# The up projection of a feed-forward layer in seven half products in place of eight, with its activations passed through memory

## What is computed

```python
def conv_ffn(xn, ffn_up, ffn_conv_w, ffn_conv_b, ffn_down):
    u = causal_depthwise_conv(xn @ ffn_up, ffn_conv_w, ffn_conv_b)
    gate, up = jnp.split(u, 2, axis=-1)
    return (jax.nn.gelu(gate, approximate=True) * up) @ ffn_down
```

## Time and profile before

| | |
|---|---|
| median of 3 runs | 3038.76 us (3037.23 to 3042.54) |
| profiled execution, its span | 3034.1 us |
| TensorE busy | 2887.8 us, 95% |
| VectorE, ScalarE, GpSimd busy | 53%, 38%, 37% |
| granted TensorE clock, mean | 0.981 |

### The profile page before, as it was taken

The page is one execution under the profiler, slowest core; times in us unless marked ns, Lnnn a source line. Parts: engine busy times, 40 slices in busy tenths (PEclk is TensorE's granted clock), DMA queues, the critical chain, the costliest instruction groups (busy, mean ns, idle before and its releaser), DMA issues.

```text
span 3034.1 us, 43412 instructions
## 1 busy us (share of the span) xinstructions
PE 2887.8 (95%) x15476; PEld 2429.7 (80%) x15476; DVE 1616.0 (53%) x2999; ACT 1160.1 (38%) x2100; POOL 1114.8 (37%) x760
## 2 busy tenths in 40 slices
PE   7999998999999999999999999999999978889999
PEld 6689867777888888887888788997878776778877
DVE  3899938343222222223039378981223849978861
ACT  3311166252222211223123356772312536767740
POOL 2223033532222225663236334335332534333234
PEclk9999997899999999999999999999999999999999
DMA  4123323431111113353856444314436763131223
GB/s 140 64 97 132 97 76 74 132 125 42 48 48 48 48 48 97 119 180 99 160 187 196 108 117 95 105 38 135 145 120 215 206 159 81 49 77 35 83 84 125
DMA packets 219008, 321.37 MB, mean 106 GB/s; under 512 B 81942, under 2 KB 152470, under 8 KB 218342
## 3 DMA queue, kind: packets, MB, share of 16 engines
q1 hardware_dynamic: 195446, 275.20, 31.5%
q10 hardware_dynamic: 22192, 39.98, 3.6%
q0 software_dynamic: 1216, 4.20, 0.5%
HBM read 227.86 MB, written 91.47 MB: 105 GB/s over the span
## 4 chain that ended last, share of the span: by engine, by line
PE 83%; DVE 6%; issue 3%; DMA 2%; ACT 2%; POOL 2%; SPq 1%; POOLq 0%; DVEq 0%; ACTq 0%
PE psum L2783 16%; PE psum L737 13%; PE psum L2568 8%; PE psum L2986 8%; PE psum L444 6%; PE psum L1275 4%; PE psum L1306 4%; PE psum L1286 3%; PE psum L530 3%; PE psum L1573 2%; PE psum L984 2%; PE psum L962 1%; DVE arena L3574 1%; PE psum L973 1%; PE psum L2033 1%
## 5 line engine op out<-in xcount | busy, mean ns | idle before, releaser
L2783 PE MATMUL psum<-parts_ffn 128*128 128x512 f32 x2112 | 482.2, 391 | 3.6 <-DVE parts_ffn L2740 3.6
L2783 PEld LDWEIGHTS psum<-parts_ffn 128*128 128x128 f32 x2112 | 398.5, 189 | 87.1 <-issue 2.2
L2853 DVE SCALAR_TENSOR_TENSOR arena<-psum,arena 128x1023 f32<-128x1023 f32 x88 | 112.9, 1282 | 329.9 <-ACT arena L2837 323.6
L737 PE MATMUL psum<-parts_even,parts_ffn 128*128 128x512 f32 (+1 forms) x1344 | 287.4, 375 | 0.0
L737 PE MATMUL psum<-parts_odd 128*128 128x496 f32 (+1 forms) x1344 | 269.2, 360 | 6.3 <-POOL parts_odd L652 5.4
L737 PEld LDWEIGHTS psum<-parts_even,parts_ffn 128*128 128x128 f32 x1344 | 238.5, 188 | 44.5
L737 PEld LDWEIGHTS psum<-parts_odd 128*128 128x128 f32 x1344 | 226.8, 191 | 41.7 <-POOL parts_odd L652 5.6
L444 PE MATMUL psum<-parts_mixer 128*128 128x512 f32 x912 | 210.4, 391 | 0.3 <-DVE parts_mixer L287 0.3
L444 PEld LDWEIGHTS psum<-parts_mixer 128*128 128x128 f32 x912 | 170.8, 188 | 35.9 <-DVE parts_mixer L287 0.5
L402 POOL CAST parts_ffn<-arena 128x1024 fp32r<-128x1024 f32 x44 | 45.8, 1042 | 355.7 <-PE psum L2783 194.6
L2311 DVE TENSOR_SCALAR_CACHE_REDUCE choose_flags<-arena,choose_bits 128x384 uint8<-128x384 f32 (+2 forms) x198 | 174.3, 942 | 1.2
(11 more groups left out here) (396 smaller groups left out, 5977.9 us busy)
## 6 DMA issues: line engine op xcount, KB each, us to landing
arena<-ffn_up_b SPq DMA_DIRECT2D x44, 512.0 KB, 3.5
arena<-ffn_down_k SPq DMA_DIRECT2D x44, 512.0 KB, 3.7
arena<-x SPq DMA_DIRECT2D x8, 2048.0 KB, 10.1
x<-arena SPq DMA_DIRECT2D x24, 512.0 KB, 4.0
arena<-w_in_e SPq DMA_DIRECT2D x24, 512.0 KB, 5.5
e_tokens<-arena ACTq DMA_DIRECT2D x24, 512.0 KB, 3.7
arena<-w_in_o SPq DMA_DIRECT2D x24, 496.0 KB, 5.9
o_tokens<-arena ACTq DMA_DIRECT2D x20, 496.0 KB, 3.5
```

Of the source, the lines that this page charges most:

```text
L737: last = pe.matmul(self.bank(t, n), self.hT[:, a, k, t * P:(t + 1) * P], w, start=(k, a, b) == (0, 0, 0), stop=(k, a) == (KT - 1, 1))
L2783: last = pe.matmul(self.core.psum[:, 4 * u + 2 * s + h, :], parts[:, s, a, k, :], self.hT[:, b, k, h * HALF:(h + 1) * HALF], start=(k, a, ...
L2853: dve.scalar_tensor_tensor(out=self.cs[:, s, lag:S], in0=src[:, 0:S - lag], scalar=self.conv_w[:, bass.ds(at * 3 + 2 - lag, 1)], in1=self. ...
```

## The change

`FfnUp` is written anew. The weights of a gate and an up tile are cut in two along k: A11 and A12 (gate), A21 and A22 (up); `hT` is cut along k and along the tokens: B11, B21 (first 512 tokens), B12, B22. The four half results C11, C12 (gate), C21, C22 (up) come from seven products of half the k length, in Winograd's form of Strassen's method: sums s1 to s4 of the weights and t1 to t4 of the activations, P1 = A11 B11, P2 = A12 B21, P3 = s4 B22, P4 = A22 t4, P5 = s1 t1, P6 = s2 t2, P7 = s3 t3. Each is 4 k tiles by three matmuls, 12 matmuls of 128x512; a pair has 84. Some are added up in PSUM (P2 on P1; P7 and P4 on P6; P3 on P5), the rest by ScalarE and VectorE into a new SBUF buffer `gu`.

The t blocks are made once, at the opening of the stage (`HalfBlocks`), in place of the plain taking out of the second half of the tokens. The sums of the weights are made for each pair: on GpSimd for the first, on VectorE for the others (`next_sums`, four additions of 128x512), and GpSimd splits seven parts of 128x512 in place of two of 128x1024. The taps read `gu` in SBUF in place of PSUM. A pair's weights (1024 KB) come in one load, and VectorE's result of 128x1024 is stored to memory (`store`, 512 KB) and read back by `FfnDown` in steps of 256 KB (`load_act`). In the loop, body r multiplies pair r (P1, P6, P5, P2, P7, P3) and P4 of pair r-1; VectorE finishes pair r-1 there and makes the sums of pair r+1. On SP, iteration r waits for the split of A22 of pair r-1, loads the weights of pair r+1, waits for the result of pair r-1 and stores it. Buffers have new places, and there are 20 more semaphores.

```diff
...
+        finish(engine, 5)
+        if ahead is not None:
+            ahead(engine)
+        for t in range(6, TT):
             finish(engine, t)
...
+class HalfBlocks:
...
+    def wait_bank(self, pe, k):
+        if k < self.Q:
+            pe.wait_ge(self.rows.low_out, 5 + k)
+        else:
+            self.wait(pe, "t1_raw", k - 4)
+    def keep_first(self, pool):
+        for k in range(KT):
+            high, low = self.first(k)
+            pool.wait_ge(self.rows.low_out, k + 1)
+            if k == self.Q:
+                pool.wait_ge(self.rows.stored[0], 16 * (TT // 2))
+            pool.tensor_tensor(self.plain("t1" if k < self.Q else "t4", k % self.Q), high.bitcast(F32), low.bitcast(F32), ALU.add).then_inc(self.by_gpsimd, 1)
...
+    def vector_second(self, dve):
+        Q = self.Q
+        for k in range(Q):
+            self.wait(dve, "held", k)
+            self.wait(dve, "raw_first", k)
+            dve.scalar_tensor_tensor(out=self.plain("t1", k), in0=self.bank(k), scalar=self.column(k), in1=self.plain("t1", k),
+                                     op0=ALU.mult, op1=ALU.subtract).then_inc(self.by_vector, 1)
+        for k in range(Q):
+            dve.wait_ge(self.rows.turned, KT + Q + k + 1)
+            self.wait(dve, "t1_raw", k)
+            dve.scalar_tensor_tensor(out=self.plain("t2", k), in0=self.bank(k), scalar=self.column(Q + k), in1=self.plain("t1", k),
+                                     op0=ALU.mult, op1=ALU.subtract).then_inc(self.by_vector, 1)
+            self.wait(dve, "t2_raw", k)
+            self.wait(dve, "raw_first", Q + k)
+            dve.tensor_tensor(self.plain("t4", k), self.plain("t4", k), self.plain("t2", k), ALU.subtract).then_inc(self.by_vector, 1)
+        for k in range(Q):
+            self.wait(dve, "t2_high", k)
+            self.wait(dve, "t4_raw", k)
+            dve.tensor_tensor(self.low("t2", k), self.plain("t2", k), self.high("t2", k).bitcast(F32), ALU.subtract).then_inc(self.by_vector, 1)
+        for k in range(Q):
+            self.wait(dve, "b22_high", k)
+            dve.scalar_tensor_tensor(out=self.plain("t3", k), in0=self.bank(k), scalar=self.column(Q + k), in1=self.plain("t3", k),
+                                     op0=ALU.mult, op1=ALU.subtract).then_inc(self.by_vector, 1)
+        for k in range(Q):
+            dve.scalar_tensor_tensor(out=self.low("b22", k), in0=self.bank(k), scalar=self.column(Q + k), in1=self.high("b22", k).bitcast(F32),
+                                     op0=ALU.mult, op1=ALU.subtract).then_inc(self.by_vector, 1)
...
 class FfnUp(Stage):
...
+    TERMS = {"p1": ("a11", "b11", 0), "p2": ("a12", "b21", 0), "p6": ("s2", "t2", 1), "p7": ("s3", "t3", 1),
+             "p4": ("a22", "t4", 1), "p5": ("s1", "t1", 2), "p3": ("s4", "b22", 2)}
+    STARTS = ("p1", "p6", "p5")
+    USER = {weight: product for product, (weight, *_) in TERMS.items()}
...
+    def bodies(self, engine, first=0):
+        for n in range(first, 2):
+            yield n, n - 1, n + 1, 0, (n + 1) // 2, n % 2, n
+        with engine.Fori(0, self.tiles // 2 - 2) as i:
+            for e in range(2):
+                yield 2 * i + (2 + e), 2 * i + (1 + e), 2 * i + (3 + e), i + 1, i + (1 + e), e, None
+        for n in range(self.tiles - 2, self.tiles):
+            yield n, n - 1, n + 1, n // 2, (n + 1) // 2, n % 2, n
+    def bank(self, n, side):
+        return self.core.psum[:, 3 * side + n, :]
...
+    def load(self, sp, r, e):
+        sp.dma_start(self.raw[e].rearrange("p (s a) f -> p s (a f)", s=2), self.w[bass.ds(2 * r, 2)].rearrange("s p f -> p s f")).then_inc(self.loaded[e], 16)
+    def load_first(self, sp):
+        hold(sp, self.retired + self.after["raw0"])
+        self.load(sp, 0, 0)
+    def store(self, sp, q, e):
+        sp.wait_ge(self.result, q + 1)
+        sp.dma_start(self.out[bass.ds(q * P, P), :], self.gu[:, e, 0]).then_inc(self.stored[e], 16)
     def sync(self, sp):
-        self.weights.load_rest(sp)
+        hold(sp, self.after["rings"])
+        self.load(sp, 1, 1)
+        for r, q, nxt, half, half_next, e, at in self.bodies(sp, 1):
+            sp.wait_ge(self.split_done["a22"], r)
+            if at == self.tiles - 1:
+                self.early.sync_early(sp)
+            else:
+                self.load(sp, nxt, 1 - e)
+            self.store(sp, q, 1 - e)
+    def store_last(self, sp):
+        self.store(sp, self.tiles - 1, (self.tiles - 1) % 2)
+    def split(self, pool, v, e, count):
+        source, high, low = self.plain(v, e), self.parts[v][:, 0], self.parts[v][:, 1]
+        pool.sem_inc(self.high_ready, 1)
+        pool.tensor_copy(high, source).then_inc(self.high_ready, 1)
+        pool.wait_ge(self.high_ready, 2 * count + 2)
+        pool.tensor_tensor(low, source, high.bitcast(F32), ALU.subtract).then_inc(self.split_done[v], 1)
...
+    def weight_sums(self, engine, e, sem, before):
+        a11, a12, a21, a22 = (self.raw[e][:, n] for n in range(4))
+        s1, s2, s4 = (self.sums[e][n] for n in ("s1", "s2", "s4"))
+        engine.tensor_tensor(s1, a21, a22, ALU.add).then_inc(sem, 1)
+        engine.wait_ge(sem, before + 1)
+        engine.tensor_tensor(a21, a11, a21, ALU.subtract).then_inc(sem, 1)
+        engine.tensor_tensor(s2, s1, a11, ALU.subtract).then_inc(sem, 1)
+        engine.wait_ge(sem, before + 3)
+        engine.tensor_tensor(s4, a12, s2, ALU.subtract).then_inc(sem, 1)
     def gpsimd(self, pool):
...
+        hold(pool, self.retired)
+        pool.wait_ge(self.loaded[0], 16)
+        self.split(pool, "a11", 0, 0)
+        self.split(pool, "a12", 0, 1)
+        self.blocks.keep_first(pool)
+        hold(pool, self.after["rings"])
+        self.weight_sums(pool, 0, self.first_sums, 0)
+        pool.wait_ge(self.first_sums, 4)
+        self.split(pool, "s2", 0, 2)
+        self.split(pool, "s1", 0, 3)
+        self.blocks.low_of_first(pool)
+        self.split(pool, "s3", 0, 4)
+        self.split(pool, "s4", 0, 5)
+        self.blocks.low_of_last(pool)
+        for r, q, nxt, half, half_next, e, at in self.bodies(pool):
+            last, count = at == self.tiles - 1, 7 * r + 6
+            if not last:
+                pool.wait_ge(self.loaded[1 - e], 16 * half_next + 16)
+                pool.wait_ge(self.used["p1"], nxt)
+                self.split(pool, "a11", 1 - e, count)
+                count = count + 1
+            if at != 0:
+                pool.wait_ge(self.used["p4"], r)
+            self.split(pool, "a22", e, count)
+            if last:
+                continue
+            pool.wait_ge(self.summed, 4 * nxt)
+            for n, v in enumerate(("s2", "s1", "a12", "s3", "s4")):
+                pool.wait_ge(self.used[self.USER[v]], nxt)
+                self.split(pool, v, 1 - e, count + (n + 1))
...
+                last = pe.matmul(self.bank(n, e), self.parts[v][:, a, k * P:(k + 1) * P], self.blocks.parts[block][b][k],
+                                 start=p in self.STARTS and (k, a, b) == (0, 0, 0), stop=(k, a) == (KT // 2 - 1, 1), skip_group_check=True)
+        last.then_inc(self.used[p], 1)
...
+            first = at == 0
+            if at not in (0, 1):
+                pe.wait_ge(self.c11_out, q)
+            self.multiply(pe, "p1", r, e)
+            if first:
+                for k in range(KT // 2):
+                    self.rows.turn(pe, 1, k)
+                pe.wait_ge(self.first_out, 1)
+                self.multiply(pe, "p2", r, e)
+                for k in range(KT // 2, KT):
+                    self.rows.turn(pe, 1, k)
+            else:
+                pe.wait_ge(self.y_out, r)
+                self.multiply(pe, "p4", q, 1 - e, opening=at == 1)
+            if at == 1:
+                hold(pe, self.blocks.banks_free)
+            if at not in (0, 1):
+                pe.wait_ge(self.c21_out, q)
+            self.multiply(pe, "p6", r, e, first)
+            if at not in (0, 1):
+                pe.wait_ge(self.c12_out, q)
+            self.multiply(pe, "p5", r, e, first)
+            if not first:
+                pe.wait_ge(self.first_out, nxt)
+                self.multiply(pe, "p2", r, e)
+            pe.wait_ge(self.x_out, nxt)
+            self.multiply(pe, "p7", r, e, first)
+            pe.wait_ge(self.fifth_out, nxt)
+            self.multiply(pe, "p3", r, e, first)
+        pe.wait_ge(self.y_out, self.tiles)
+        self.multiply(pe, "p4", self.tiles - 1, 1)
...
+            self.take_first(act, r, q, nxt, e, at)
+            self.tap(act, 0, q, r, 1 - e, at)
+            self.gelu(act, r)
+            self.tap(act, 1, q, r, 1 - e, at)
+            self.take_fifth(act, r, nxt, e, at)
+            self.take_c11(act, nxt, half, e, at)
...
+    def take_x(self, dve, nxt, half, e, at):
+        if at not in (0, 1):
+            dve.wait_ge(self.stored[e], 16 * half)
+        dve.wait_ge(self.first_out, nxt)
+        dve.wait_ge(self.used["p6"], nxt)
```

(81 more changed lines are left out.)

376 lines of the change are left out of this document (232 added, 144 removed).

## The result

| | before | after |
|---|---|---|
| median, same chip and series | 3037.99 us (3036.11 to 3042.54, 4 runs) | 3090.65 us (3086.37 to 3098.9, 4 runs) |
| ratio, 95% interval | | 1.0181 (1.0153 to 1.0209) |
| profiled execution, its span | 3034.1 us | 3090.9 us |
| first up matmul to first down matmul | 488.9 us | 541.2 us |
| down projection | 243.7 us | 250.9 us |

The change makes the kernel 1.8% slower. The forecast was 3076 us, 37 more than before; the medians differ by 52.7. The difference of the spans, 56.8 us, lies in the up projection (52.3) and the down projection (7.2); the rest of the kernel, the same code, gave 2.7 back.

The account below looks back on a forecast made before the run. The prediction took TensorE alone to bound the up projection before the change; after it, opening 46.5, circles 439 and tail 40.5 make 526 us against 488.9, 37 more: span 3071, median 3076 us, range 3008 to 3106.

Parts of the forecast that it names:

- The circle: Up projection loop: result, store, load, sums, next result form one closed circle of 16.6 + 6.5 = 23.1 us a pair.
- TensorE's slack in the circle: Up projection loop: TensorE, needing 19.2 us a pair, idles 3.9 us ahead of P7, which waits for x.
- rival 3: Up projection loop: heavier waits of 5.5 and load of 7, 25.1 us a pair, 3114 us; lower TensorE clock; chance 0.13.
- Waits between VectorE and GpSimd: Up projection loop: alternating on SBUF work, the two engines bring the result 4.0 us later, 16.6 after the landing.
- Rival 1: Up projection loop: engines meet little, load quick, TensorE bounds at 19.2 to 20 us a pair, 3000 us; chance 0.14.
- the page's rule: Loop's shared SBUF ports: first issuer blocks the other fully, which would cost 1.4 us a pair more.
- The load's half: Loop, result to landing: semaphore 0.2, store's issue 0.4, load 5.9, together 6.5 us; bounds 5.2 and 7.5.
- The opening: Start of the up projection: pair 2's load lands 46.5 us after the first matmul; P6 starts at 696.
- The tail and the down projection: After the last landing: 38.5 us to P4's end, about 2 more waiting for C21, together 40.5.
- the last result's store: Down projection: this store holds the loads from step 4 on, 21 us added up, costing nothing, at most 3.
- rival 2: Up projection loop: milder waits of 2.0 to 2.5, load 5.5, 20 to 21.9 us a pair, 3017 to 3053; chance 0.21.
- The point from which it decides: Up projection loop: at 21.15 us a pair the stage takes its earlier 488.9 us.

Follow-up runs that it names:

- e1_lag: The changed kernel with SP loading the next pair before any wait for VectorE and storing each result one iteration later: 3028.29 us, ratio 0.9971.
- e3_wait: As e1_lag, but SP waits for the result ahead of the load again and issues the store behind it: 3084.52 us, ratio 1.0148.
- e2_short: The changed kernel with GpSimd's subtractions in the loop covering 64 of 512 columns, SP's order kept: 3025.97 us.
- e5_tail_open: e1_lag with t4's low parts behind two weight splits at the opening and C21 taken ahead of the last gate taps: 3028.84 us, ratio 0.997.
- e7_last_store: e6 with the last pair's store issued behind the loads of the down projection's steps 3 to 6: 3014.24 us, ratio 0.9936.
- e6: e5_tail_open with ScalarE making the weights' high parts in the loop, GpSimd only the subtractions: 3018.97 us, ratio 0.9946.
- e4: The changed kernel with the edits of e1_lag and e2_short together: 3020.46 us.

## Why the prediction was right, and where its sizes were off

**The circle.** The forecast rested on one closed circle, result to store to load to sums to result, of 16.6 + 6.5 = 23.1 us a pair. Measured: 17.0 + 6.4, 23.39. The schedule behind the 16.6 holds along the way too: behind the landing at 865.18, x is there after 11.1 us (10.95 forecast) and the result after 17.2. That it is a circle and not TensorE, VectorE or the load alone, the runs show from three sides. Cut at SP (e1_lag), it falls to 20.0 though each engine does the same work. Closed again with the store out of the way (e3_wait), it is 23.05. Shortened in its other half (e2_short), it falls to 19.6 though the wait stays.

TensorE's slack in the circle, put at 3.9 us of idle a pair, is 3.83 (23.39 less 19.56), but it idles only 2.35 of them. The other 1.5 go into matmuls at a lower granted clock (last section), which is what rival 3 feared; they ate slack and did not lengthen the circle.

**Waits between VectorE and GpSimd, 4.0 us of the 16.6.** Alone, the chain was put at 12.6. With subtractions of 64 columns it is 13.45, and casts are still there; so the long subtractions are worth 3.6 us, and the mutual waiting was the term to have. I had the GpSimd subtraction at 1.09 us; here it takes 1.27 to 1.29 where VectorE is not in its way. That can make up the 0.4 by which the 16.6 was short; it was not tried by itself. Rival 1, with little meeting of the engines, fell here.

The Trainium skill ("SBUF — State Buffer", "Who interferes with whom") has one engine keep the shared ports for its whole instruction; it writes this of VectorE's two-port modes, and of an operation with two SBUF inputs only that it contends with a GpSimd instruction that reads SBUF. For the additions of this loop the trace agrees in the main: VectorE's addition issued at 866.81 ended only at 868.59, 0.54 after the subtraction that ended at 868.05. But 0.54 is less than its 0.69, so it got on 0.15 us before the other's end, as in the earlier trace rows. With 1.4 us a pair more, which the page's rule would have made, a pair would have been 24.5; it was 23.39.

**The load's half, 6.5 us.** Measured 6.1 to 6.7, 6.35 on average. Its parts were off both ways: a load of 1 MB behind a store landed in 5.2 to 5.9 us, 5.4 on average, where I took 5.9, and 4.8 with no store ahead; the load was issued 0.74 to 1.12 us behind the result, 0.9 on average, where I took 0.6. A store landed in 2.7 to 3.1. So a part of the pair's closeness, 23.39 for 23.1, is luck: 0.4 too little in one half, 0.15 too much in the other.

**The opening, 46.5 us: mis-sized.** It took 55.9. I had left a piece out: four low parts of t4 on GpSimd stand ahead of the splits of A11(1) and A22(0), on which P1 and the load of pair 2 wait. P6, too, was late, at 699.70 for 696: VectorE's low parts of t2 took 5.45 us for four (2.8 forecast), beside GpSimd's low parts of t1 (6.73 for four) and the splits of s3 and s4.

```profile
699.70 8.19 PE L3043 MATMUL psum<-parts_ffn,up_s 128*128 128x512 f32 x24 [10.75 <-DVE parts_ffn L2876]
...
709.20 6.23 POOL L2899 TENSOR_TENSOR up_t<-arena,up_t 128x512 fp32r<-128x512 f32 x4 [8.51 <-ACT up_t L2856]
...
717.38 4.57 PE L3043 MATMUL psum<-parts_ffn,up_a 128*128 128x512 f32 x12 [3.08 <-POOL up_a L2990]
...
719.27 0.38 SPq L2960 DMA_DIRECT2D arena<-ffn_up_b  x1
...
724.10 1.45 DVE L2996 TENSOR_TENSOR arena<-arena 128x512 f32<-128x512 f32 x1 [9.07 <-DMA arena<-ffn_up_b]
```

These lines of the changed kernel's timeline answer to the earlier trace rows. In e5_tail_open, without the piece, the stall of 3.1 us is gone and the weight sums of pair 2 begin 46.9 us behind the first up matmul, in e1_lag 55.6. So the piece has 8.7 of the 9.4 us; P6 is as late there as here.

**The tail and the down projection.** From the last landing to the first down matmul it took 40.9 us, where the forecast had 38.5 and 2 more of stall for C21 inside the down projection; that stall was 4.60. The granted clock has a part in both. Behind its last wait for x (3.41 us) P7 and P3 of pair 20 took 7.06 us at a mean clock of 0.78, where 5.7 is usual, and TensorE ran without a wait from there to the down projection. Behind the stall for C21, 36 matmuls took 9.91 us at 0.83 (1216.91 to 1226.82), where the same 36 of e5_tail_open, behind its 1.29, took 8.29 at 1.00:

```profile
1216.91 10.07 PE L3342 MATMUL psum<-down_parts 128*128 128x512 f32 x36 [4.60 <-DVE arena L3162]
```

So of the down projection's 7.2 us more, 4.6 are the stall, 1.6 the clock behind it, and 1.0 remain, as in e7_last_store (244.7 for 243.7), which has no such stall. I had put the last result's store at 0 to 3 us for the loads of step 4. In the changed kernel the stall at C21 covers it; once that was gone it was 5.41 (e5) and 4.87 (e6), and e7 shows its cause. The 21 us that I had added up for it were 29.1 in e5: the result came 15.3 us behind P4's end for 11, and the first two loads behind the store took 6.3 and 6.6 us to land for 3.6.

**The balance.** Opening 9.4, circles 5.4, tail 0.4, down projection 7.2, less 2.5 behind it and 0.2 ahead: 19.7 of the 19.9 us by which the span missed the 3071 that was forecast. So the change was forecast at 37 us and came to 57, and a third of it was not in the sum.

**Two slips in the sums.** With waits of 2.5 and a load of 5.5 rival 2 ends at 20.6 us a pair, not 21.9. And 19 pairs of 22 to 24.1 us give 3055 to 3095, not 3057 to 3097. The measured 3090.65 lies in either range.

**The point from which it decides.** I had put it at 21.15 us a pair. With the opening, tail and down projection as measured it is (488.9 + 2.5 - 7.2 - 55.9 - 40.9) / 19 = 20.4. e1_lag with 20.0 lies just under it, and its ratio just under 1.

**Where the expected gain went.** TensorE loses 12 of 96 matmuls a pair. The first loss is in the matmuls: 84 of them take 19.56 us without a gap, 0.2329 each, where I used 0.2283; it costs 0.38 us a pair, 8 in all. In the opening TensorE idles 21 us (55.93 less 34.51), at a mean granted clock of 0.73. So without the circle this form of the stage takes 463 to 465 us (e2, e4, e6 and e7) against 488.9, not the 450 of rival 1. Of the 77 us by which the changed kernel's 541.2 lie above 464, the circle has 73, 19 times 3.83.

## What to carry to other kernels

When a change puts a wait for a late result into an in-order DMA queue, look for what is queued behind it and whether that feeds the same result: a closed circle adds latencies that no engine's busy share shows. Here the cure was to issue the load first and the store one iteration late. Where VectorE's operations have two inputs in SBUF, price each meeting with a GpSimd operation at that operation's remaining length. After each repair look for what is late next, as e5 and e7 did: in e5 two right edits brought 3.4 us of 9, because they handed the rest to the next wait.
